# Moving a bias from a VectorE add into one-row matmuls, in a fused two-block transformer kernel

## The reference, cut to what matters

```python
z = jax.nn.gelu(xc)
u, v = jnp.split(z, 2, axis=-1)
v = layernorm(v, ln_g, ln_b).reshape(B, L // CHUNK, CHUNK, N_GMLP_HEADS, GMLP_HEAD_DIM)
g = jnp.einsum('bnpec,eqp->bnqec', v, w_s) + b_s.T[:, :, None]      # chunks of 128, 6 heads of 128
return u * g.reshape(B, L, D_GMLP)
```

## Time and profile before

| | us |
|---|---|
| median of 3 runs | 2461.68 |
| lowest and highest of them | 2457.25, 2462.62 |
| the profiled execution | 2457.25 |
| its span, first to last instruction | 2455.6 |
| TensorE busy in the span | 2390.4 (97%) |
| VectorE busy | 1537.6 (63%) |
| ScalarE busy | 1135.0 (46%) |
| mean granted TensorE clock | 0.993 of full |

### The profile page before, as it was taken

One profiled execution on the slowest core, in us unless ns is written; L12 is line 12 of the kernel. 1 busy time (PEld: TensorE's weight loads), 2 busy tenths in 40 slices (PEclk: granted clock), 3 DMA queues, 4 the chain that ended last, 5 costly groups with the idle time before them and its releaser, 6 DMA issues.

```text
span 2455.6 us, 50705 instructions
## 1 busy us (share of the span) xinstructions
PE 2390.4 (97%) x19936; PEld 2356.4 (96%) x19936; DVE 1537.6 (63%) x2070; ACT 1135.0 (46%) x1463; POOL 12.8 (1%) x27
## 2 busy tenths in 40 slices
PE   6999999999999999997899999999999999999999
PEld 6898999999999999996899999999999999999999
DVE  6556776676546676567876666766576455545554
ACT  5343445555435555434444445444465444444443
POOL 0000000000000000000000000000000000000000
PEclk9999999999999999998999999999999999999999
DMA  6453565555555555553333333333355355555554
GB/s 233 145 186 114 171 191 182 188 187 188 189 189 189 188 187 186 187 188 121 115 122 115 111 107 123 123 111 115 127 174 172 129 185 187 188 188 184 193 188 162
DMA packets 110191, 400.71 MB, mean 163 GB/s; under 512 B 12379, under 2 KB 12406, under 8 KB 109953
## 3 DMA queue, kind: packets, MB, share of 16 engines
q1 hardware_dynamic: 108000, 391.00, 48.2%
q0 software_dynamic: 2080, 8.06, 1.0%
HBM read 396.91 MB, written 2.10 MB: 162 GB/s over the span
## 4 chain that ended last, share of the span: by engine, by line
PE 92%; DVE 5%; issue 1%; ACT 1%; DMA 0%; DVEq 0%; SPq 0%; ACTq 0%
PE bank L420 91%; DVE w_lo L1345 1%; ACT w_hi L918 1%; DVE scratch L1394 1%; PE bank L621 1%; DVE s_k L1394 0%; DMA x<-in_xT 0%; DVE h_lo L1391 0%; DVE cum L1391 0%; DVE ping L1391 0%; DVE s_t L1391 0%; DVE root L1433 0%; DVE qr L1876 0%; DVE acc L1391 0%; DVE s_t L1398 0%
## 5 line engine op out<-in xcount | busy, mean ns | idle before, releaser
L1345 DVE TENSOR_TENSOR w_lo<-raw,w_hi 128x1024 fp32r<-128x1024 f32 x736 | 896.2, 1224 | 773.3 <-ACT w_hi L918 768.2
L918 ACT ACTIVATE w_hi<-raw 128x1024 fp32r<-128x1024 f32 x736 | 778.3, 1060 | 1073.3 <-PE bank L420 1053.0
L420 PE MATMUL bank<-h_hi,w_hi 128*128 128x256 f32 x4016 | 1146.5, 285 | 19.8 <-issue 8.3
L420 PE MATMUL bank<-h_lo,w_hi 128*128 128x256 f32 x4016 | 1124.5, 280 | 0.0
L420 PE MATMUL bank<-h_hi,w_lo 128*128 128x256 f32 x4016 | 1123.7, 280 | 0.0
L420 PEld LDWEIGHTS bank<-h_hi,w_hi 128*128 128x128 f32 x4016 | 758.9, 189 | 28.5 <-issue 14.6
L420 PEld LDWEIGHTS bank<-h_lo,w_hi 128*128 128x128 f32 x4016 | 759.1, 189 | 2.9 <-issue 1.9
L420 PEld LDWEIGHTS bank<-h_hi,w_lo 128*128 128x128 f32 x4016 | 758.2, 189 | 0.0
L420 PE MATMUL bank<-m_hi,w_hi 128*128 128x256 f32 x704 | 196.5, 279 | 0.0
L420 PE MATMUL bank<-m_lo,w_hi 128*128 128x256 f32 x704 | 196.5, 279 | 0.0
L420 PE MATMUL bank<-m_hi,w_lo 128*128 128x256 f32 x704 | 196.5, 279 | 0.0
(11 more groups left out here) (412 smaller groups left out, 2749.4 us busy)
## 6 DMA issues: line engine op xcount, KB each, us to landing
raw<-in_units SPq DMA_DIRECT2D x736, 512.0 KB, 3.3
x<-in_xT SPq DMA_DIRECT2D x4, 512.0 KB, 5.8
memx<-in_memT POOLq DMA_DIRECT2D x4, 512.0 KB, 7.3
out_y<-obuf SPq DMA_DIRECT2D x8, 256.0 KB, 4.2
bias_t<-in_bias POOLq DMA_DIRECT2D x8, 192.0 KB, 2.9
dft<-in_dft POOLq DMA_DIRECT2D x1, 1024.0 KB, 7.7
decay<-in_decay POOLq DMA_DIRECT2D x1, 768.0 KB, 5.8
con<-in_con SPq DMA_DIRECT2D x1, 546.0 KB, 8.0
```

The costliest lines, as they stand in the source:

```text
L420: return pe.matmul(out, lhsT, rhs, start=start, stop=stop, skip_group_check=True)
L918: return act.activation(out, in_, ACT.Copy, scale=scale)
L1345: dve.tensor_tensor(w_lo[slot][:, :, :], raw[slot][:, :, :], w_hi[slot][:, :, :].bitcast(F32), ALU.subtract).then_inc(split_done, 1)
```

## The change

The bias is no longer added on VectorE. For each of the 12 head-and-chunk regions a second matmul follows the `gvt` x `ws` one and accumulates onto it: its stationary operand is one row of 128 ones (partition 0 of "ones"), its moving operand one row of 128 bias values. `bs` becomes one row of 768 values on partition 0, loaded by a plain DMA of 3 KB beside `ws` and `pw`. `gated()` loses its two adds and the wait behind them, and its multiply reads the PSUM bank itself.

```diff
-        bs = place("bs", [P, HY, P], 99 * K)
+        bs = place("bs", [1, HY * P], 99 * K)
...
-            for dst, src in ((ws[:, :, :], "ws"), (pw[:, :, :], "pw")):
+            for dst, src in ((ws[:, :, :], "ws"), (pw[:, :, :], "pw"), (bs[:, :], "bs")):
                 pool.dma_start(dst, a[src]).then_inc(mixer_in, 16)
-            pool.dma_start(bs[:, :, :].rearrange("p e q -> p (e q)"), a["bs"].broadcast_to([P, HY * P]))\
-                .then_inc(mixer_in, 16)
...
             for e in range(HY):
                 for c in range(2):
                     o = banks[3 + e // 2][:, (e % 2) * T + c * P:(e % 2) * T + (c + 1) * P]
-                    m = mm(o, gvt[:, c, e * P:(e + 1) * P], ws[:, e, :])
+                    mm(o, gvt[:, c, e * P:(e + 1) * P], ws[:, e, :], True, False)
+                    m = mm(o, con[0:1, CC["ones"][0]:CC["ones"][0] + P], bs[0:1, e * P:(e + 1) * P], False, True)
                 if e % 2:
                     m.then_inc(psum_for_dve, 1)
...
             def gated(k, last=None):
                 s = 2 * (k % 2)
-                for i in range(2):
-                    step(tt(y_part[:, s + i, :].rearrange("p (c q) -> p c q", c=2),
-                            banks[3 + k][:, i * T:(i + 1) * T].rearrange("p (c q) -> p c q", c=2),
-                            bcast(bs[:, 2 * k + i, :], 2), ALU.add))
-                settle()
-                to_act(tt(y_part[:, s:s + 2, :], y_part[:, s:s + 2, :], gu[:, 2 * k:2 * k + 2, :], ALU.mult))
+                to_act(tt(y_part[:, s:s + 2, :], gu[:, 2 * k:2 * k + 2, :],
+                          banks[3 + k][:, :].rearrange("p (s t) -> p s t", s=2), ALU.mult))
```

## The result

The changed kernel takes 2473.03 us in the median of 5 runs (2470.55 to 2479.15), the kernel before 2461.68 (2457.25 to 2463.76, 5 runs). The ratio is 1.0057, 95% interval 1.0042 to 1.0074: 14 us slower, where 7.4 were forecast. The two medians of five stand only 11.35 us apart; the record has more launches of the changed kernel (eleven with the profiled one, 2470.55 to 2479.26, median 2476.86), and by the ratio the time is 2461.68 x 1.0057 = 2475.7 us. The direction was right, the size half of what came: 2475.7 lies above the range, though the median of the five lies in it.

The account below looks back on a forecast made before the run. The prediction took TensorE to bound the kernel, VectorE's saving being worth 0. Passes of 2.7 us and crossings of 4.7 us made 7.4 us, added to the median 2461.68 for 2469.1 us; range 2460 to 2474.

Parts of the forecast that it names:

- TensorE is the bound, and VectorE's saving is worth 0: Around gated(): TensorE never waits, so the 2.4 us VectorE saves over three calls lie under its work; gain 0.
- 24 passes cost 2.7 us: Twelve added float32 bias matmuls among the ws ones: 24 passes at 0.112 us each, 2.7 us, the floor.
- A crossing costs 0.20 us: At each row-count change between ws and bias matmuls a weight load starts 0.20 us late; 24 crossings cost 4.7 us.
- Rival 1: At the 24 changes between 128 rows and one, no crossing is charged: 2.7 us slower, 2464.4 us; chance 0.17.
- What is late next: After the bias matmuls, pool matmuls, group(0) and output projection start 7.4 us later; VectorE waits for TensorE, nobody for VectorE.
- Rival 2: One-row matmuls in the ws stretch also lower the clock, adding 3.4 us: 10.8 us slower, 2472.5 us; chance 0.08.
- The Trainium skill on idleness: Cited against rival 2: only idleness throttles TensorE, so the clock stays up among the one-row matmuls.
- Rival 3: The clock dip at 1106 to 1128 us goes away, saving 3.8 us: net 3.6 us slower, 2465.3 us; chance 0.08.
- The sum: Whole kernel: median 2461.68 us plus 7.4 gives 2469.1 us, 0.30% slower.

Follow-up runs that it names:

- the VectorE half alone: Kernel before with gated() multiplying from PSUM without its two adds and no bias matmul, so the bias is left out; ratio 1.0000.
- the stretch with 128 rows: First ws or bs matmul to the output projection, in the changed kernel with bias matmuls zero-padded to 128 rows; 18.3 us, ratio 0.9998 to the kernel before.
- the stretch with 64 rows: First ws or bs matmul to the output projection, in the changed kernel with bias matmuls zero-padded to 64 rows; 22.9 us, ratio 1.0024 to the kernel before.
- four one-row runs: Changed kernel with its 12 one-row matmuls issued four times in a row ahead of the ws matmuls, 96 passes; one launch, the passes took 17.7 us.
- four 128-row runs: Changed kernel with the 12 bias matmuls, zero-padded to 128 rows, issued four times ahead of the ws matmuls; one launch, clock 1.00 throughout, no ratio given.

## Why the prediction was right, and where it failed

- *TensorE is the bound, and VectorE's saving is worth 0.* Right: 1.0000 for the VectorE half alone, and the same 15.6 us in the stretch.
- *24 passes cost 2.7 us.* Right: +2.7 us in the stretch with 128 rows.
- *A crossing costs 0.20 us, 24 of them 4.7 us, 7.4 in all.* Right, and for one row too: 0.83 us a pair in the changed kernel's full-clock part, against 0.84 worked out, and +7.3 us in the stretch with 64 rows. Rows of 33 and 64 were a good price for a row count that the trace did not have. Rival 1, no crossings for one row, fell, and with it the sum that goes by the small-K rule of the Trainium skill's "TensorE: Matmul & The Clock Gate" (its table on why this matters for your kernels) alone. The rule itself holds for the passes in a run: 24 one-row passes took 2.87 us to the next start. The drain that "TensorEngine Tiling (Array Packing)", Key Properties, of the Trainium skill speaks of agrees with what the trace shows at each crossing, a weight load that starts 0.20 us late.
- *What is late next.* Right in kind: VectorE waits for TensorE, and TensorE for nobody.
- *The clock.* Here it failed, in two steps. Rival 2 is what happened, and it had a chance of 0.08. The argument against it was that 64-row matmuls ran at 1.00 at 1138 us; that carried the price of a crossing from 64 rows to one, rightly, and the clock's behaviour with it, wrongly. In the same place 64 rows hold the clock, 32 and one do not. The eight passes at 1138 us could not have shown a fall in any case: they are over in about 1.1 us, and the one-row matmuls ran for 3 us before the clock fell. The trace before did hold a sign, the 0.53 at 66 us among 64-row passes, which the prediction saw and gave little weight; with 128 rows there the clock stayed at 1.00 over a longer idle stretch. The second step is the price: 3.4 us was half of the 6.8 us dip at 66 us. But here the one-row matmuls go on, and the low clock went on with them and beyond, for 17 us, and slowed everything in it. The term that was mis-sized is the clock's: 14.9 - 7.3 = **7.6 us** in the profiled execution (13.4 - 7.3 = 6.1 in the second one, with 13.7 us of low clock) instead of 0 in the forecast and 3.4 in the rival. That rival 2's time, 2472.5 us, lies near the median of five is no merit of its price.
- *The Trainium skill on idleness.* Its "TensorE: Matmul & The Clock Gate", Part 1, names idleness as what takes the clock to its lower level, and by it the clock would have stayed up. The measurement decides against it: in 96 one-row passes without a gap the clock fell to 0.50.
- *Rival 3*, a later dip that goes away, did not come: after the stretch the changed kernel gained nothing (+0.9, +7.0, +0.7 us). The dip of 1106 us is there in the changed kernel too, some 20 us later (0.81 from 1120 to 1140 us and 0.77 from 1140 to 1160).
- *The sum.* With 13.4 to 14.9 us in the stretch the change is accounted for: the two ratios give 14.0 and 0.0068 x 2463.76 = 16.8 us, and their intervals, 10.3 to 18.2 and 11.8 to 21.4 us, hold both. What is left between them may be the step of long runs of matmuls, below; it is likely also part of why single executions of one kernel lie up to 15 us apart (the kernel before: 2458.06 to 2473.42 on one occasion). Neither was shown.

Open: what it is in the number of rows that the chip counts. The padded rows were zero in the moving operand, so it is not the values of the bias rows; the rows of the weight load and of the matmul were always changed together; rows between 32 and 64 were not tried. Rows and idle time may also count together: 64 rows held in alternation and in a run but not with the idle 1.85 us, and 32 rows were run only in alternation, with its late loads, never in a run without gaps.

## What to carry to other kernels

Where TensorE is the bound, an add on VectorE that lies under it is free, and moving it into matmuls costs in full. Price such a matmul in three parts: its passes, 0.20 us for each change of the row count next to it, and the clock; few-row matmuls belong in one short run (the stretch at +4.7 us here instead of +14.9), or are padded with zero rows to 128 (+2.7). A busy PE with few rows can be a PE that is losing its clock: look at the granted clock behind every group of small-row matmuls, also in the kernel that you start from.

## What the runs showed that was not expected

- The clock falls to 0.50 under a TensorE that never reads as idle, if its matmuls have one row (in a run without gaps too) or, alternating with 128-row ones, 32 rows; it fell 3 to 5 us after the first of them. It holds with 64 or 128 rows, but not where the 64-row passes of the kernel before have an idle 1.85 us between them.
- At full clock a long run of the same matmuls has one of two steps: the 6292 of the feed-forward took 734.7 or 741.7 us (116.8 or 117.9 ns each), the last 4256 took 501.4 or about 506.3 to 507.7. Of the eleven profiled executions other than that of the kernel before, four had the long value in the first run (the changed kernel, 64 rows, four one-row runs, four 128-row runs), five in the second. The changed kernel had the long value in its first execution and the short one in its second, so it goes by the execution and not by the program. The kernel before has one profile, with the short value in both runs; the VectorE half alone, whose TensorE program is the same, had the long one in its second. Within a run the step did not change: every 100 us inside it hold 859 to 860 matmuls or 851 to 852. What picks it was not found. It is worth up to 7 us, as much as all that was predicted here, so a difference of this size between two single profiles says nothing until the steps are compared.
